# A two-block transformer on one core: the first groups of the MLP taken by pairs of chunks, finer waits at the projections, and the modulation rows of layer 1 placed around the transposes of x

## The reference, cut to what matters

```python
mod = c_act @ ada_w[l] + ada_b[l]                       # 1024 -> 6 * 1024
sh1, sc1, gt1, sh2, sc2, gt2 = split(mod, 6)
h = rms_norm(x, norm1_g[l]) * (1.0 + sc1) + sh1
proj = h @ w_in[l]                                      # attention and delta-rule inputs, gates
...
x = x + gt1 * (merged @ w_out[l])
h = rms_norm(x, norm2_g[l]) * (1.0 + sc2) + sh2
x = x + gt2 * (square(relu(h @ w_mlp1[l])) @ w_mlp2[l]) # 1024 -> 4096 -> 1024
```

## Time and profile before

| what | us |
|---|---|
| median of 3 runs | 2444.82 |
| lowest and highest | 2435.34, 2449.72 |
| the profiled execution, its own time | 2427.97 |
| its span | 2426.5 |
| TensorE busy in the span | 1936.9 |

### The profile page before, as it was taken

How to read it: one execution, slowest core, us unless ns; L and a number is a source line. 1 busy time by engine, 2 the same in 40 slices (tenths; PEclk the granted TensorE clock), 3 DMA queues, 4 the chain that set the end, 5 groups by cost and what they waited for, 6 DMA issues and landing times.

```text
span 2426.5 us, 30450 instructions
## 1 busy us (share of the span) xinstructions
PE 1936.9 (80%) x12595; PEld 1237.2 (51%) x12595; DVE 871.9 (36%) x1476; ACT 599.1 (25%) x1056; POOL 46.3 (2%) x45
## 2 busy tenths in 40 slices
PE   4989998998989998998897866666687987666665
PEld 2867775986867885986654311111155542111111
DVE  2655443655655344654573200000046530000001
ACT  2233203544333203543361100000034410000000
POOL 0000100000000100000000000000000000000000
PEclk8999999999999998999988988888898988888888
DMA  9344234653335243554417999999973579999996
GB/s 355 143 166 181 104 141 166 254 202 142 139 139 194 76 165 125 191 191 109 165 68 286 409 409 409 409 409 410 409 227 140 213 305 409 409 409 409 409 409 273
DMA packets 189428, 617.46 MB, mean 254 GB/s; under 512 B 20913, under 2 KB 23787, under 8 KB 183019
## 3 DMA queue, kind: packets, MB, share of 16 engines
q1 hardware_dynamic: 184592, 611.61, 65.5%
q10 hardware_dynamic: 4698, 3.90, 0.6%
HBM read 614.44 MB, written 1.05 MB: 254 GB/s over the span
## 4 chain that ended last, share of the span: by engine, by line
PE 50%; SPq 24%; DMA 10%; DVE 9%; ACT 4%; issue 2%; ACTq 1%; POOL 0%; DVEq 0%
PE pb L564 47%; SPq L2592 24%; DMA ring<-in_w_up_dram 4%; PE pb L567 3%; DMA ar<-in_w_up_dram 2%; DVE ar L1371 2%; DMA ring<-in_w_down_dram 2%; ACT ar L2083 2%; DVE ar L1379 2%; DMA hT<-in_w_up_dram 2%; DVE wp L1371 1%; DVE small L1387 1%; DMA rows<-in_swa_sink_dram 1%; ACT ar L2087 1%; DVE ar L1375 0%
## 5 line engine op out<-in xcount | busy, mean ns | idle before, releaser
L564 PE MATMUL pb<-ring,ar 128*32 128x512 f32 (+2 forms) x2320 | 381.1, 702 | 202.7 <-DMA ring<-in_w_up_dram 154.6
L564 PE MATMUL pb<-ar 64*64 64x64 f32 (+10 forms) x3736 | 430.3, 366 | 108.6 <-DMA hT<-in_w_up_dram 37.8
L2087 ACT COPY ar<-pb 128x512 f32<-128x512 f32 (+2 forms) x195 | 112.6, 578 | 1078.0 <-PE pb L564 1005.1
L564 PEld LDWEIGHTS pb<-ar 64*64 64x64 f32 (+4 forms) x3736 | 217.5, 145 | 311.1 <-issue 167.7
L1383 DVE COPY ar<-pb 128x512 f32<-128x512 f32 (+5 forms) x98 | 58.7, 599 | 817.3 <-PE pb L564 800.3
L564 PEld LDWEIGHTS pb<-ring,ar 128*32 128x32 f32 (+1 forms) x2320 | 99.1, 127 | 454.4 <-issue 205.8
L564 PE MATMUL pb<-hT,ring 128*128 128x256 f32 x1024 | 237.2, 390 | 0.0
L564 PEld LDWEIGHTS pb<-hT,ring 128*128 128x128 f32 x1024 | 197.8, 196 | 32.0 <-issue 4.0
L1371 DVE TENSOR_TENSOR ws<-ring,ws 128x1024 fp32r<-128x1024 f32 x128 | 156.9, 1226 | 142.0 <-ACT ws L2087 141.0
L564 PE MATMUL pb<-hs,ws 128*128 128x256 f32 x1536 | 189.9, 287 | 13.3 <-DVE hs L1371 13.3
L564 PEld LDWEIGHTS pb<-hs,ws 128*128 128x128 f32 x1536 | 188.6, 196 | 17.4 <-issue 17.4
(11 more groups left out here) (146 smaller groups left out, 1392.1 us busy)
## 6 DMA issues: line engine op xcount, KB each, us to landing
ring<-in_w_down_dram SPq DMA_DIRECT2D x48, 2048.0 KB, 21.6
ring<-in_w_gate_dram SPq DMA_DIRECT2D x86, 1024.0 KB, 18.7
ring<-in_w_up_dram SPq DMA_DIRECT2D x86, 1024.0 KB, 18.7
ring<-in_w_mlp_dram SPq DMA_DIRECT2D x32, 2048.0 KB, 7.8
ring<-in_w_in_dram SPq DMA_DIRECT2D x28, 2048.0 KB, 10.6
ring<-in_ada_w_dram SPq DMA_DIRECT2D x24, 2048.0 KB, 7.6
ar<-in_w_gate_dram SPq DMA_DIRECT2D x42, 1024.0 KB, 18.4
ar<-in_w_up_dram SPq DMA_DIRECT2D x24, 1024.0 KB, 18.5
```

The costliest lines, as they stand in the source:

```text
L564: return e.matmul(o, l, r, start=start, stop=stop)
L2087: return e.copy(o, i)
```

## The change

**Ring order.** Blocks 0 and 1 of group 0 of layer 1's modulation weights now stand ahead of layer 0's `w_mlp1` block 0, and blocks 2 and 3 ahead of block 1. Blocks 0 and 1 of group 1 stand ahead of layer 1's `w_in` block 0, blocks 2 and 3 ahead of block 1. `sync` waits for parameters and constants before its fourth block, not its second.

**Rows.** `ada_ahead` is gone. In layer 0 two rows of group 0 stand on TensorE between `acc_out` and the transposes of x for the MLP, two behind the transposes; in layer 1 two rows of group 1 stand ahead of the transposes for site "a", two behind. The transposes of group 0 stand behind MLP group 9, those of group 1 behind projection group 4. The steps r 0 to r 4 of layer 1's mix are empty.

**MLP.** Groups 0 and 2 run pair by pair, each with its own waits for the high and the low part of h; then group 1, then 3 to 31.

**Projections.** TensorE waits for w_hi and h_hi, then for w_lo, then for h_lo, each ahead of the pass that reads it. VectorE makes hT of pair 0 ahead of w_lo of group 0; ScalarE casts pair 0 of h ahead of making hT of pair 1.

```diff
@@ ring order
+                if l and j < 2:
+                    for i in (2 * j, 2 * j + 1):
+                        ada(1, 1, i)
                 cols(("win", l, j), a["w_in"][l], 512 * j, 512)
...
-                if step == "r" and n % 5 < 4:
+                if step == "r" and n % 5 < 4 and (l == 0 or n > 4):
...
             for j in range(8):
+                if l == 0 and j < 2:
+                    for i in (2 * j, 2 * j + 1):
+                        ada(1, 0, i)
                 cols(("mlp1", l, j), a["w_mlp1"][l], 512 * j, 512)
-                if l == 0 and j < 4:
-                    ada(1, 0, j)
@@ tensor: lin3, group(g)
-                    if j == 0:
-                        e.wait_ge(*V("h_lo", site, l, q))
-                    e.wait_ge(*V("w_lo", site, l, g))
+                    e.wait_ge(*A("w_hi", site, l, g))
                     hi, lo = [v4(z[:, 0:2 * n], 2) for z in wp[g % 2]]
-                    for t in range(2):
-                        u = 0
-                        for w, h in ((hi, 0), (lo, 0), (hi, 1)):
+                    for u, (w, h) in enumerate(((hi, 0), (lo, 0), (hi, 1))):
+                        if j == 0 and u != 1:
+                            e.wait_ge(*(V("h_lo", site, l, q) if u else A("h_hi", site, l, q)))
+                        if u == 1:
+                            e.wait_ge(*V("w_lo", site, l, g))
+                        for t in range(2):
                             for c2 in range(2):
...
@@ tensor: mlp(l)
-                turned("n2", l, turn("n2", l, None))
...
+                if l == 0:
+                    for i in range(2):
+                        ada_row(1, 0, i)
+                ks = turn("n2", l, None)
+                if l == 0:
+                    for i in range(2, 4):
+                        ada_row(1, 0, i)
+                turned("n2", l, ks)
...
+                for cp in range(4):
+                    e.wait_ge(*A("h_hi", "n2", l, cp))
+                    for g in (0, 2):
+                        up_(g, (2 * cp, 2 * cp + 1), (0, 1))
+                    e.wait_ge(*V("h_lo", "n2", l, cp))
+                    for g in (0, 2):
+                        m = up_(g, (2 * cp, 2 * cp + 1), (2,))
+                        if cp == 3:
+                            m.then_inc(*P.up("mlp1", l, g))
+                for g in (1, *range(3, 32)):
...
+                    if l == 0 and g == 9:
+                        ada_col(1, 0, aux[:, 0:512])
@@ tensor: block1(l), layer 1
+                    for i in range(2):
+                        ada_row(1, 1, i)
                     ks = turn("n1", l, None)
+                    for i in range(2, 4):
+                        ada_row(1, 1, i)
...
+                    if l and g == 4:
+                        ada_col(1, 1, room1[1])
@@ vector: lin3
+                hT_of(0)
                 low(0)
-                for cp in range(4):
-                    if cp % 2 == 0:
-                        hT_of(cp)
-                    if cp:
-                        h_low(cp - 1)
-                h_low(3)
+                h_low(0)
+                hT_of(2)
+                for cp in range(1, 4):
+                    h_low(cp)
@@ scalar: lin3
                 high(0)
-                for cp in range(4):
-                    if cp % 2:
-                        hT_of(cp)
-                    if cp:
-                        h_high(cp - 1)
+                h_high(0)
+                hT_of(1)
+                h_high(1)
+                hT_of(3)
+                h_high(2)
                 h_high(3)
                 high(1)
@@ sync
-                if i == 1:
+                if i == 3:
                     e.wait_ge(*D("par"))
                     e.wait_ge(*D("c1"))
```

More of the change, by code:

```diff
@@ L614, in r @@
                 g, i = 1 + n // 5, n % 5
+                if l and g == 1:
+                    return
                 if i < 4:
@@ new lines, in mlp, with up_ @@
+                ks = turn("n2", l, None)
[3 more added lines that the diff above has]
+                turned("n2", l, ks)
+                def up_(g, cs, passes):
+                    hi, lo = [v4(z, 8) for z in wsp[g % 3]]
+                    o = banks[psum.at["mlp1", l, g // 2]][:, 256 * (g % 2):256 * (g % 2) + 256]
+                    for q in passes:
+                        for c in cs:
+                            m = mm(o, (hi, lo, hi)[q][:, c, :], hs[q // 2][:, c, :], q == 0 and c == 0, q == 2 and c == 7)
+                    return m
@@ new lines, in mlp @@
+                for g in (0, 2):
+                    bank("mlp1", l, g // 2)
+                    e.wait_ge(*V("cut", l, g))
+                for cp in range(4):
[3 more added lines that the diff above has]
+                    e.wait_ge(*V("h_lo", "n2", l, cp))
+                    for g in (0, 2):
+                        m = up_(g, (2 * cp, 2 * cp + 1), (2,))
+                        if cp == 3:
+                            m.then_inc(*P.up("mlp1", l, g))
@@ L994, in mlp @@
+                for g in (1, *range(3, 32)):
+                    if g % 2 == 0:
+                        bank("mlp1", l, g // 2)
+                    e.wait_ge(*V("cut", l, g))
+                    up_(g, range(8), (0, 1, 2)).then_inc(*P.up("mlp1", l, g))
+                    if l == 0 and g == 9:
+                        ada_col(1, 0, aux[:, 0:512])
                     if g % 2:
-                        psum.until(held[0], A, "relu", l, g // 2)
+                        psum.until(psum.at["mlp1", l, g // 2], A, "relu", l, g // 2)
@@ L1025, in mlp @@
                     psum.until(ks[n][0], V, "x", "mlp", l, n)
[L1027 to L1032, removed]
             def block1(l):
@@ L1736, in r @@
             def r(l, n):
-                if n % 5 == 4:
+                if n % 5 == 4 and (l == 0 or n > 4):
                     mod(l, 1 + n // 5)
@@ L1761, in cut @@
             def cut(l, g):
-                if l == 0 and g == 24:
+                if l == 0 and g == 16:
                     mod(1, 0)
@@ L1807, in block1 @@
                 modT = modT2[l]
-                normed("n1", l, ("x0", 0) if l == 0 else ("mlp", 0))
                 if l == 0:
+                    normed("n1", l, ("x0", 0))
                     mod(0, 0)
@@ L1812, in block1 @@
                 tt(sa1[:, :], S("sc1", 8), pcol(pl["n1"], 8), ALU.mult).then_inc(*V.up("sa1", l))
+                if l:
+                    normed("n1", l, ("mlp", 0))
                 group = lin3("a", l, [512, 512, 512], [P("ada_col", 0, 0) if l == 0 else P("acc", "mlp", 0, 3)], ahead(l),
@@ L1816, in block1 @@
                     group(g)
+                    if l and g == 5:
+                        mod(1, 1)
                 e.wait_ge(*P("lin", "a", l, 11))
@@ L2126, in ada_row @@
             def ada_row(l, g, room):
-                if g:
-                    e.wait_ge(*(P("ya", l, 1) if g == 1 else P("ada_col", l, 1)))
+                if l == 0 and g == 1:
+                    e.wait_ge(*P("ya", 0, 1))
+                if g == 2:
+                    e.wait_ge(*P("ya", l, 1))
+                    e.wait_ge(*P("ada_col", l, 1))
                 e.wait_ge(*P("ada_row", l, g, 3))
@@ L2132, in r @@
             def r(l, n):
-                if n % 5 == 3:
+                if n % 5 == 3 and (l == 0 or n > 4):
                     ada_row(l, 1 + n // 5, room1[1 + n // 5])
@@ L2318, in cut @@
             def cut(l, g):
-                if l == 0 and g == 16:
+                if l == 0 and g == 8:
                     ada_row(1, 0, aux[:, 0:512])
@@ L2379, in block1 @@
                              lambda cp: hT_out("n1", l, cp, lambda c: sa1[:, c:c + 1], lambda c: modT2[l][:, c:c + 1], lambda cc: hT3[:, cc, :]))
+                if l:
+                    ada_row(1, 1, room1[1])
                 for g in range(12):
```

19 lines of the change are left out of this document (1 added, 18 removed).

## The result

| | before | changed |
|---|---|---|
| median of the runs (lowest to highest) | 2445.2 us (2435.3 to 2449.7, 4 runs) | 2405.18 us (2401.88 to 2415.07, 4 runs) |
| ratio, 95% interval | | 0.9848 (0.9807 to 0.989) |
| profiled execution: own time, span | 2427.97, 2426.5 | 2415.07, 2413.6 |

The changed kernel is 40 us faster by the medians, 32.5 were forecast, and 2405 lies 7 under the 2412.3 that was given. The two profiled executions, however, differ by only 12.9 us. That is the second thing to explain.

The account below looks back on a forecast made before the run. TensorE bound the MLP and DMA engines the expert stage, with TensorE idle at seams; 5.5 + 12.7 + 5.0 + 2.5 + 1.0 + 3.8 + 2.0 = 32.5 off the median 2444.82 gave 2412.3 us, range 2399 to 2430.

Parts of the forecast that it names:

- MLP of layer 1: Layer 1's MLP: TensorE starts products at about 942.9 instead of 949.26; 5.5 us gained (4.2 to 6.9).
- MLP of layer 0: Layer 0's MLP: groups end earlier and three rows leave a full TensorE; 12.7 us gained (10 to 14).
- the earlier groups: Layer 0's MLP: first three groups end at 402.7 instead of 409.6; 6.9 us gained.
- Projections: Projections "b" of both layers and "a" of layer 0: earlier matmuls through reordered casts and waits; 2.5 us gained each.
- the 3.3 of my step: Projections "b": casting pair 0 first starts TensorE at about 1141.3 instead of 1144.58.
- Projection "a" of layer 1 and its mix: Layer 1: the projection ends earlier, 1.0 us gained; four rows leave the mix, 3.8 gained (0 to 7.7).
- Start: Kernel start: two early SyncE blocks leave ScalarE's late parameters alone sooner; 2 us gained, bounds 6 gained to 6 lost.
- My second rival: Kernel start: parameters and x land late, the first row starts 6 us later; total 2420.3 us, chance 0.12.
- The first rival: At the seams: the clock stays at 1.2 GHz, TensorE starts earlier but slowly; total 2420.6 us, chance 0.24.
- Slower, or no effect: Whole kernel: MLP out of step, 2482 us, chance 0.04; or moved matmuls wait elsewhere, within 0.5%, chance 0.03.
- the third rival: MLP, both layers: later groups wait for their cuts, 70 us lost, 2482 us; decides above 0.56 a group; chance 0.04.

Follow-up runs that it names:

- second profiles: The kernel before and the changed kernel, each run and profiled once more with nothing changed: 2443.04 us and 2411.47 us.

## Why the prediction was right in its time, and where it was not

The time came within 7 us of the forecast, well inside the range. That it came so near is luck, because two errors stood against each other: the edits are worth 25.5, not 32.5, and the medians moved by 14 more than the edits are worth. The 7 that the edits lack are the start, which lost 5 or more instead of gaining 2; the other terms together came out near their 30.5, the finer waits above their forecast, the rows and the pairs below it.

*MLP of layer 1*, forecast 5.5: measured 5.2 (108.5 to 103.3; 5.9 by the second profiles). The middle between a low and a high clock was right: the clock came up on the way, 24 matmuls at 142 ns each (3.40/24) and 96 at 123.

*MLP of layer 0*, forecast 12.7: measured 12.0 (117.1 to 105.1). I had the rows at 5.8 and the earlier groups at 6.9. Rows alone give 8.0 here (14.2 and 94.9 for 14.6 and 102.5), since all four leave the full TensorE and also fill the gap ahead of the transposes; the pairs then add 4.0. The missing 0.7 is less than the new stall at 422.54.

*Projections*, forecast 2.5 + 2.5 + 2.5 + 1.0 = 8.5: the finer waits measured 12.0 and 14.1. TensorE starts 3.2 us earlier at both "b" (4.2 us behind the down product instead of 7.4 in layer 0), nearly the 3.3 of my step. I then let low clock and the late w_lo take back all but 1.4 to 2.9, and took 2.5. Nothing of the kind in layer 1: there, from the end of the projection of layer 0 to the end of this one, 3.7 and 4.0 stay in the changed kernel and 4.4 with the waits alone; in layer 0 1.7, 4.3 and 2.7, as its projection takes 53.7 to 56.3 by the clock. The 413 ns that I took for the low level are a mix, too: the mean granted clock of that group is 0.57. The value taken, 2.5, was the mis-sized term. At "a" of layer 0 the kernel with the waits alone starts at 46.69 instead of 50.87 and is 3.7 and 4.7 ahead at the scan, where I had 2.5.

*Projection "a" of layer 1 and its mix*, forecast 1.0 + 3.8: the stretch from the down product to the scan is 5.9 and 3.3 shorter. Of it, from the projection's end to the scan, 4.2 and 1.6 (2.4 with the rows alone) stand for the 3.8. The rows alone give 2.0 in it and the waits alone 0.1; with the rows around the transposes, TensorE gets to the projection at full clock (1.00 from 594.40 to 604), and the projection ends 1.7 us earlier after the down product, which neither part gives alone (0.2 at most).

*Start*, forecast +2.0 (6 to either side): it lost 7.4 by cleared span, 5.8 of it at the scan already (244.4 for 238.6), and 5.0 there by the means of all profiles. This step failed, sign and all. I argued from 24 to 28 us, where SyncE's large packets delay the small ones, and took the two blocks as something that would then be out of the way. I did not ask what ran from 12 to 16 us, while SyncE stood at its wait: ScalarE's queue alone, at 812 packets in 4 us. The wait was the cover of the small loads, and the change took it away. The late parameter did wait less (10.10 for 14.10), but ScalarE issued it 7.9 later. My second rival had this mechanism, at 6 lost; its total of 2420.3 was too high because the medians moved by more than the edits are worth.

*The clock.* The first rival said that it would stay low. It did at the transposes of layer 1's MLP (3.65 us, granted clock 0.50) and not where products stand ahead (1.94 us at 1.00, in the changed kernel and with the rows alone); and in layer 1 it rose during the first 24 matmuls. The Trainium skill, "TensorE: Matmul & The Clock Gate", Part 4, says that transposes do not engage the full clock. These rows show 16 of them at it, 121 ns each, when TensorE came to them from products after an idle time of 0.96 us; the rule of the Trainium skill does not hold there. Behind gaps of 3.00 to 6.56 us they took 2.42 to 3.65.

*Slower, or no effect:* after the first groups no wait repeats. `pb<-hs,ws` has 4.1 us of idle time in all 1536 matmuls of the changed kernel, where the third rival asked for more than 32:

```profile
L568 PE MATMUL pb<-hs,ws 128*128 128x256 f32 x1536 | 186.3, 284 | 4.1 <-ACT hs L2112 1.6
```

*The step from the profile to the median.* I subtracted the sum from the median as though both stood on the same ground. They do not: before's median has two falls in the scan (about 16 over its cleared time), the changed kernel's about one, or none. 25.5 of the 40 us are the edits. The other 14 must lie in how often and how long the clock fell, if the cleared spans are right, but only one part of this is seen: in all seven profiles that have the rows moved and the scan as it was, layer 1's scan takes 72.6 to 75.8. In the five others in which it fell it takes 77.4 to 78.2, and in one it did not fall. It is 1.6 to 4.8 us shorter than 77.4 wherever the four rows have left layer 1's mix. In the profile with 72.6 the stretch ahead of the scan is 2.6 longer instead, so not all of that is a gain. It does not cover 14. Whether the rest is a changed chance of a fall, and why this should depend on edits hundreds of microseconds away, is not shown: with one or two profiles of each kernel the runs cannot be sorted one by one. It is open.

**The best kernel** is the change with SyncE's wait left at its second block: 2402.93 by median, 7.4 under the changed kernel by cleared span, 5.0 by the arrival at the first scan. Its ratio to before is 0.9837 (0.9813 to 0.9861); against the changed kernel's runs (2401.88 to 2415.07) the medians differ by 2.3, less than they scatter, so there it rests on the profiles.

## What to carry to other kernels

A seam is worth filling from both ends: independent matmuls ahead of and between the transposes (they also bring them to full clock), and the first products taken in the order in which their operands arrive. Before a wait ahead of bulk loads is loosened, look at what else uses the DMA engines while it holds: it may be what lets the small loads through. And before a sum from a profile is set against a median, profile the kernel twice and compare the stages that nobody touched.

## What the hardware showed that I had not expected

- One kernel's scan takes 70.9 or 77.4 us with the same instructions, by the granted clock alone (1.00 or 0.89), in either layer. The runs of the same kernel spread over 2426.5 to 2445.4, in three heaps. More matmuls beside the gaps did not stop it (77.8 and 81.0); filled gaps were not tried.
- Where both queues had work in these profiles, they shared by count of packets, not bytes: 181 and 181 in 4 us, with 1.42 and 0.22 MB, and 207 and 207 with 1.69 and 0.01. The Trainium skill, "DMA: Bandwidth & Descriptors", Queues, rings and completion order, has them alternate by packets of some 9 to 17 descriptors; by it I had put the loss at 10 us. The equal counts fit the alternation; how many descriptors a packet of these rows holds no run shows. The loss was 5.0 to 7.4.
- The issuing engine was held as well while the two queues shared: from 10.8 to 24.7 us ScalarE's issues took 1.08 to 3.65 us each, and so its first work came at 27.14 instead of 19.12.
